# Two halves of the tokens at the first block's first inner norm: a front chain beside the back's last products

## The reference, cut to what matters

```python
mix = jnp.einsum('bsd,de->bse', merged, w_out)
x = x + rmsnorm(mix, g_post_mix)          # the first inner norm
h2 = rmsnorm(x, g_pre_mlp)
a = jnp.square(jax.nn.relu(jnp.einsum('bsd,df->bsf', h2, w_up)))
```

## Time and profile before

| | us |
|---|---|
| median of 3 runs (1938.03 to 1939.36) | 1939.18 |
| the profiled execution's own time | 1938.89 |
| its span, first to last instruction | 1937.2 |
| TensorE (PE) busy in the span | 1902.5 (98%) |
| VectorE (DVE) busy | 1132.7 (58%) |
| ScalarE (ACT) busy | 908.8 (47%) |
| GpSimd (POOL) busy | 85.3 (4%) |

### The profile page before, as it was taken

The page is one execution under the profiler, slowest core; times in us unless marked ns, Lnnn a source line. Parts: engine busy times, 40 slices in busy tenths (PEclk is TensorE's granted clock), DMA queues, the critical chain, the costliest instruction groups (busy, mean ns, idle before and its releaser), DMA issues.

```text
span 1937.2 us, 27051 instructions
## 1 busy us (share of the span) xinstructions
PE 1902.5 (98%) x9061; PEld 1518.7 (78%) x9061; DVE 1132.7 (58%) x1916; ACT 908.8 (47%) x1649; POOL 85.3 (4%) x120
## 2 busy tenths in 40 slices
PE   8999999899999989999999999999999999999998
PEld 7878778688888868757888888888856788888887
DVE  5656566744333357667576656436567667666634
ACT  5555573444433334556544334334466644334433
POOL 2111000000000000110010000000020020000000
PEclk9999999999999999999999999999999999999999
DMA  4222223232333322531233333233441133333222
GB/s 144 66 65 71 66 76 98 65 106 95 98 98 97 95 79 73 115 79 34 82 93 93 98 99 98 95 97 93 109 95 46 41 91 98 103 95 95 93 98 103
DMA packets 169190, 171.29 MB, mean 88 GB/s; under 512 B 48546, under 2 KB 123280, under 8 KB 169104
## 3 DMA queue, kind: packets, MB, share of 16 engines
q1 hardware_dynamic: 169000, 170.14, 30.4%
q10 hardware_dynamic: 104, 0.03, 0.0%
HBM read 159.24 MB, written 2.10 MB: 83 GB/s over the span
## 4 chain that ended last, share of the span: by engine, by line
PE 88%; DVE 6%; ACT 3%; issue 1%; DMA 1%; SPq 0%; POOL 0%; DVEq 0%; ACTq 0%; POOLq 0%
PE bank_b L2185 15%; PE bank_b L2187 15%; PE bank_b L2186 15%; PE bank_a L2185 13%; PE bank_a L2187 12%; PE bank_a L2186 12%; PE bank_b L2559 2%; PE bank_a L2312 1%; PE bank_b L2662 1%; PE bank_a L2643 1%; DVE w_lo L1407 1%; DVE arena L1407 1%; DVE arena L1410 1%; DVE h_lo L1410 0%; DVE x_t L1407 0%
## 5 line engine op out<-in xcount | busy, mean ns | idle before, releaser
L1407 DVE TENSOR_TENSOR w_lo<-w_raw,w_hi 128x512 fp32r<-128x512 f32 (+3 forms) x621 | 414.8, 680 | 584.3 <-ACT w_hi L1124 370.2
L1124 ACT ACTIVATE w_hi<-w_raw 128x512 fp32r<-128x512 f32 (+3 forms) x396 | 233.4, 599 | 441.1 <-PE bank_b L2187 227.2
L2185 PE MATMUL bank_b<-h_hi,w_hi 128*128 128x512 f32 x944 | 371.0, 393 | 1.6 <-DVE w_lo L1407 1.4
L2186 PE MATMUL bank_b<-h_lo,w_hi 128*128 128x512 f32 x944 | 367.7, 390 | 0.0
L2187 PE MATMUL bank_b<-h_hi,w_lo 128*128 128x512 f32 x944 | 367.7, 389 | 0.0
L2185 PE MATMUL bank_a<-h_hi,w_hi 128*128 128x512 f32 x592 | 233.8, 395 | 15.2 <-DVE h_lo L1410 14.3
L829 ACT ACTIVATE w_hi<-w_raw 128x512 fp32r<-128x512 f32 x225 | 137.8, 627 | 232.1 <-PE bank_b L2187 118.6
L2186 PE MATMUL bank_a<-h_lo,w_hi 128*128 128x512 f32 x592 | 232.1, 392 | 0.0
L2187 PE MATMUL bank_a<-h_hi,w_lo 128*128 128x512 f32 x592 | 231.8, 392 | 0.0
L2185 PEld LDWEIGHTS bank_b<-h_hi,w_hi 128*128 128x128 f32 x944 | 177.2, 188 | 40.8 <-issue 3.6
L2186 PEld LDWEIGHTS bank_b<-h_lo,w_hi 128*128 128x128 f32 x944 | 177.2, 188 | 37.2 <-issue 1.4
(11 more groups left out here) (279 smaller groups left out, 2570.0 us busy)
## 6 DMA issues: line engine op xcount, KB each, us to landing
w_raw<-in_w_up_dram SPq DMA_DIRECT2D x240, 256.0 KB, 3.1
w_raw<-in_w_down_dram SPq DMA_DIRECT2D x152, 256.0 KB, 2.6
arena<-arena SPq DMA_DIRECT2D x32, 268.0 KB, 4.3
w_raw<-in_w_in_dram SPq DMA_DIRECT2D x64, 128.0 KB, 2.3
w_raw<-in_w_gate_dram SPq DMA_DIRECT2D x32, 256.0 KB, 2.8
w_raw<-in_w_in_dram SPq DMA_DIRECT2D x32, 256.0 KB, 2.6
w_raw<-in_w_o_dram SPq DMA_DIRECT2D x32, 256.0 KB, 2.6
w_raw<-in_w_out_dram SPq DMA_DIRECT2D x16, 256.0 KB, 2.8
```

The costliest lines, as they stand in the source:

```text
L1124: nc.scalar.activation(w_hi[:, s, 0:c], w_raw[:, s, 0:c], ACT.Copy).then_inc(w_round, 1)
L1407: return nc.vector.tensor_tensor(out_, a, b, op)
L2185: nc.tensor.matmul(out_, a_hi, b_hi, start=start, stop=False, skip_group_check=loose)
L2186: nc.tensor.matmul(out_, a_hi, b_lo, start=False, stop=False, skip_group_check=loose)
```

## The change

The first 256 tokens (front) and the last 256 (back) get a chain of their own. In the second half of the output projection each product of 512 tokens becomes two of 256; `bank_b` is laid out so that banks 0 and 1 hold the front of the four tiles and banks 2 and 3 the back. In the last two chunks the four front pieces come first, then one back piece, the front's sum of squares in three products with ones of 256 columns, then the three other back pieces and the back's sum in five such products. The first group of the up projection takes each chunk as a front and a back half; tiles 0 and 1 of the front stand ahead of tiles 0 and 1 of the back, from tile 2 on both halves follow each other and DVE and ACT work on the whole tile. ACT takes over the variance from DVE. The first three additions of the new squares go from DVE to POOL.

```diff
@@ layout @@
+FRONT, BACK = slice(0, S // 2), slice(S // 2, S)
+        mix_parts_b = bank_b[:, :, :].rearrange("p (h a) n -> p h (a n)", h=2).rearrange("p h (j n) -> p h j n", j=4)
@@ gpsimd @@
+            pool.wait_ge(stat_ready, 1)
+            for t in range(1, 4):
+                pool.wait_ge(sq_ready, KT + t + 1)
+                pool.wait_ge(sq_added, KT - 1 + t - 1)
+                nc.gpsimd.tensor_tensor(ssum[:, :], x_sq[:, 0, :] if t == 1 else ssum[:, :], x_sq[:, t, :],
+                                        ALU.add).then_inc(sq_added, 1)
@@ scalar @@
-            post_squares(range(4, KT), 0, N_UP - 1, 0, 0)
...
+            act.wait_ge(sq_added, 3)
+            for a in range(2):
+                act.wait_ge(front_made, a + 1)
+                nc.scalar.activation(sq[:, a, :], bank_b[:, a, :], ACT.Square).then_inc(front_sq, 1)
+            act.wait_ge(front_stat, 1)
+            act.wait_ge(eps_set, 1)
+            ln_of(FRONT, front_ln)
+            act.wait_ge(front_ln, 1)
+            guess_of(FRONT, front_guess)
+            var_of(FRONT, front_var)
+            act.wait_ge(post_made, 1)
+            nc.scalar.activation(sq[:, 2, :], bank_b[:, 2, :], ACT.Square).then_inc(sq_ready, 2)
+            act.wait_ge(w_used, N_UP)
+            nc.scalar.activation(sq[:, 3, :], bank_b[:, 3, :], ACT.Square).then_inc(sq_ready, 2)
+            round_new(0, FRONT, front_new, front_round)
+            act.wait_ge(stat_ready, 1)
+            ln_of(BACK, ln_ready)
+            act.wait_ge(ln_ready, 1)
+            guess_of(BACK, guess_ready)
+            var_of(BACK, var_ready)
+            round_new(1, FRONT, front_new, front_round)
             split1(N_UP + 2)
-            post_guess(1)
             split1(N_UP + 3)
...
+            for f in range(2):
+                round_new(f, BACK, x_new1, xg_round)
+            for f in range(2):
+                x_square(f)
+            for f in range(2, KT):
+                round_new(f, slice(0, S), x_new1, xg_round)
                 if 3 <= f < KT - 1:
                     split1(N_UP + f + 1)
                 x_square(f)
@@ vector @@
...
+            for f in range(4, 6):
+                add_front(f)
+            dve.wait_ge(front_guess, 1)
+            tt(rs0[:, FRONT], rs1[:, FRONT], rs1[:, FRONT], ALU.mult).then_inc(front_newton, 1)
...
+            inc_new(0, FRONT, front_inc)
+            add_new(0, FRONT, front_inc, front_new)
+            inc_new(1, FRONT, front_inc)
+            lo_new(0, FRONT, front_round, front_ready)
+            add_new(1, FRONT, front_inc, front_new)
+            dve.wait_ge(guess_ready, 1)
...
+            for f in range(2, KT):
+                add_new(f, slice(0, S), xinc_ready, x_new1)
+                if f + 1 < KT:
+                    inc_new(f + 1, slice(0, S), xinc_ready)
+                lo_new(f, slice(0, S), xg_round, xg_ready)
+                if f < KT - 1:
+                    split_lo(N_UP + f + 1)
+            for t in range(4, KT):
+                add_square(t, KT, KT - 1, 1, True)
@@ tensor @@
+            def mix_part(chunks, j, c):
+                r = slice(j * P, j * P + P)
+                for k in chunks:
+                    s = (N_OUT + KT + k) % SLOTS
+                    last = mm3(mix_parts_b[:, 0 if c == FRONT else 1, j, :], w_hi[:, s, r], w_lo[:, s, r], h_hi[:, k, c], h_lo[:, k, c],
+                               k == 0 and j % 2 == 0, k == KT - 1, True)
...
+                mix_part(two, 0, FRONT)
+                mix_part(two, 1, FRONT).then_inc(front_made, 1)
+                mix_part(two, 2, FRONT)
+                mix_part(two, 3, FRONT).then_inc(front_made, 1)
+                mix_part(two, 0, BACK)
+                pe.wait_ge(mix_out, 1)
+                pe.wait_ge(front_added, 2)
+                of_squares(ssum[:, FRONT], FRONT, True, False)
+                pe.wait_ge(front_sq, 2)
+                of_squares(sq[:, 1, FRONT], FRONT, False, False)
+                of_squares(sq[:, 1, BACK], FRONT, False, True).then_inc(front_stat, 1)
+                mix_part(two, 1, BACK).then_inc(post_made, 1)
+                mix_part(two, 2, BACK)
+                mix_part(two, 3, BACK)
...
+            def up1_parts():
...
+                for k in range(2):
+                    pe.wait_ge(front_ready, k + 1)
+                    up_part((N_UP + k) % SLOTS, k, FRONT)
+                for k in range(2):
+                    pe.wait_ge(xg_ready, k + 1)
+                    up_part((N_UP + k) % SLOTS, k, BACK).then_inc(w_used, 1)
+                for k in range(2, KT):
+                    s = use(N_UP + k)
+                    pe.wait_ge(xg_ready, k + 1)
+                    up_part(s, k, FRONT)
+                    up_part(s, k, BACK).then_inc(w_used, 1)
```

More of the change, by code:

```diff
@@ new lines, in round_new @@
+            def round_new(f, c, new, made):
+                act.wait_ge(new, f + 1)
+                nc.scalar.activation(h_hi[:, f, c], x_t[:, f, c], ACT.Copy,
+                                     scale=cols1[:, C_PMLP + f:C_PMLP + f + 1]).then_inc(made, 1)
+            act.wait_ge(sq_added, 3)
[3 more added lines that the diff above has]
+            act.wait_ge(front_stat, 1)
@@ new lines, in lo_new @@
+            def lo_new(f, c, rounded, made):
+                dve.wait_ge(rounded, f + 1)
+                stt(h_lo[:, f, c], x_t[:, f, c], cols1[:, C_PMLP + f:C_PMLP + f + 1],
+                    h_hi[:, f, c].bitcast(F32), ALU.mult, ALU.subtract).then_inc(made, 1)
+            for f in range(4, 6):
+                add_front(f)
+            dve.wait_ge(front_guess, 1)
+            tt(rs0[:, FRONT], rs1[:, FRONT], rs1[:, FRONT], ALU.mult).then_inc(front_newton, 1)
+            dve.wait_ge(front_newton, 1)
@@ L2227, in total_squares, with up_part @@
                     of_last(False).then_inc(stat_ready, 1)
+            def up_part(s, k, c):
+                for j in (0, 2, 3, 1):
+                    if k == 0 and j == 1 and c == FRONT:
+                        pe.wait_ge(ln_ready, 1)
+                        pe.wait_ge(var_ready, 1)
+                    r = slice(j * P, j * P + P)
+                    last = mm3(bank_a[:, j, c], w_hi[:, s, r], w_lo[:, s, r], h_hi[:, k, c], h_lo[:, k, c], k == 0 and c == FRONT,
+                               k == KT - 1, True)
+                return last
@@ new lines, in mix_end, with of_squares @@
+            def mix_end():
+                def of_squares(src, c, start, stop):
+                    return nc.tensor.matmul(bank_a[:, 0 if c == FRONT else 1, c], ones[:, :], src, start=start, stop=stop)
+                two = range(KT - 2, KT)
+                use(N_UP - 1)
+                mix_part(two, 0, FRONT)
[12 more added lines that the diff above has]
+                mix_part(two, 3, BACK)
+                pe.wait_ge(mix_out, 2)
+                pe.wait_ge(sq_added, 3)
+                of_squares(ssum[:, BACK], BACK, True, False).then_inc(sq_added, 1)
+                for a in range(2):
+                    pe.wait_ge(sq_ready, 6 + 2 * a)
+                    for c in (FRONT, BACK):
+                        last = of_squares(sq[:, 2 + a, c], BACK, False, a == 1 and c == BACK)
+                        if a == 1 and c == BACK:
+                            last.then_inc(stat_ready, 1)
+                        else:
+                            last.then_inc(sq_added, 1)
@@ L2416, in _ @@
                     pe.wait_ge(merge_split, k + 1)
[L2417 to L2420, removed]
+                    if half == 0:
+                        wide(bank_a, s, h_hi[:, k, :], h_lo[:, k, :], k == 0, k == KT - 1)
+                    else:
+                        for j in range(4):
+                            mix_part([k], j, FRONT)
+                        for j in range(4):
+                            last = mix_part([k], j, BACK)
+                        last.then_inc(w_used, 1)
+            mix_end()
+            def up1_parts():
+                use(N_UP + 1)
+                pe.wait_ge(mix_out, 4)
+                pe.wait_ge(front_ln, 1)
+                pe.wait_ge(front_var, 1)
+                for k in range(2):
[9 more added lines that the diff above has]
+                    up_part(s, k, BACK).then_inc(w_used, 1)
             def up1(set_, g, i=0, gper=0, late=None):
```

83 lines of the change are left out of this document (65 added, 18 removed).

## The result

| | before | changed |
|---|---|---|
| median of 20 runs, us | 1938.83 | 1942.02 |
| lowest to highest | 1937.12 to 1939.42 | 1940.16 to 1942.79 |
| profiled execution, its span | 1937.2 | 1940.2 |

The ratio is 1.0017 with a 95% interval of 1.0011 to 1.0023: the change costs 3.2 us. The forecast was 1939.6, its range ended at 1942.0. The range missed by 0.02, and the forecast itself by 2.4 us.

What follows compares the result with a forecast made beforehand. PE, busy 98% of the span, was taken as the bound. Old wait and slow clock -9.5, added work +4.3, remaining waits +5.6 gave +0.4 us: median 1939.6, range 1936.4 to 1942.0.

Steps and rivals of the forecast that it cites:

- from there PE bounds the rest as before: After the up projection's first group, nothing more shifts; the stage's +0.4 us carries through to the end.
- SP's load of chunk 6: In the changed stage: moves some 9 us later with a weight split, lands in 3.1, wanted over 8 later, costs nothing.
- The stage itself: Output projection's second half to the up projection's first group's end: +0.4 us in all.
- Halves at 0.120: PE's 256-column products in the changed stage start 0.120 us apart; 192 halved products add 2.56 us of work.
- Rival 2: Halved products in the changed stage cost half, 0.1135 us: -1.4 us, or 1937.8; chance 0.15.
- rival 4: Weight load no longer hides behind 256 columns: 0.168 us a product, 18 us more, 1958; chance 0.05.
- The front chain hidden behind the back's pieces: At the norm, PE's three pieces and five sums cover the front's chain, which uncovered would cost 4.4 us.
- The waits: PE's remaining waits from the norm through the up projection's first group: six terms, 5.6 us together.
- POOL's additions stop DVE: In the up projection's first group, additions on POOL stretch DVE's two-SBUF-input steps, one stop of 1.05 us each.
- rival 1: POOL's additions miss DVE's two-input steps in the first group: -2.1 us, or 1937.1; chance 0.20.
- rival 3: Clock falls to half in the 3.1 us wait before the third chunk: +2.0 us, or 1941.2; chance 0.10.

Runs made afterwards that it cites:

- e12: Kernel before, with PE's code behind the second norm placed at slot 61 of a page of 256; median 1940.73 us against 1938.88.
- e6: Kernel before, with PE's code behind the second norm placed at slot 0 of a page of 256; median 1939.14 us, ratio to before 1.0004.
- e8: Kernel before, with PE's code behind the second norm placed at slot 128 of a page of 256; median 1938.96 us, ratio to before 1.0003.
- e5: Changed kernel, with PE's code behind the second norm placed at slot 0 of a page of 256; median 1940.25 us, ratio to before 1.0011.
- e7: Changed kernel, with PE's code behind the second norm placed at slot 128 of a page of 256; median 1940.28 us, ratio to before 1.0011.
- e2: Changed kernel plus 36 empty PE instructions (semaphore increments) at the second norm; median 1940.35 us, ratio to before 1.0010.
- e1: Changed kernel plus 104 empty PE instructions (semaphore increments) at the second norm; median 1947.0 us, ratio to before 1.0042.
- e4: Like e1, but with the three additions on POOL back on DVE; median 1945.81 us against 1947.0.
- e9: Like e7, but with the three additions on POOL back on DVE; median 1938.55 us, ratio to before 0.9999.

## Why the prediction was wrong

**The term that failed** is the last step of its sum: "from there PE bounds the rest as before". The code there is the same, but not its place. PE's program was 408 instructions longer, its code was loaded at other times, and two of these loads fell on SP while SP's issues set the pace of the second block. That is 1.14 + 0.81 = 1.95 us in the profiles, 1.85 when before alone is put there (e12). No rival named it. "SP's load of chunk 6" was the only place where the prediction looked at SP at all.

**The stage itself** was walked rightly in its mechanism: +0.69 against +0.4 in this pair of profiles. Over the five profiles with the change (88.54 to 89.21) and the four with before's code in this stage (before, e6, e8, e12: 87.85 to 88.54) the means are 0.85 apart, twice the forecast. In part the near sum is luck: PE's waits are 4.7 in total and not 5.6, but the half behind each wait holds up the next by 0.19 to 0.23 in place of 0.12, which was in no term.

- Halves at 0.120: measured 0.119 to 0.120. Rival 2 (0.1135) and rival 4 (the weight load shows) fell. The Trainium skill's page "TensorE: Matmul & The Clock Gate", section "Back-to-back issue gap", gives its 2.5 ns for a product by itself; for these pairs of weight load and product it is too small, the halving costs 12 to 13 ns.
- The front chain hidden behind the back's pieces: yes. PE goes on at 360.53, which is 360.25 in before's count of time, against 360.03.
- The waits, 0.1, 0.3, 0.6, 0.8, 3.1 and 0.7 forecast: 0.24, under 0.1 (the view doesn't list it), 0.27, 0.64, 2.92 and 0.61 measured.
- POOL's additions stop DVE (rival 1 fell): 1.75 to 1.78 a step, 1.05 a stop as taken. The Trainium skill's page "SBUF — State Buffer", section "SBUF: two separate sides", says that such a DVE step and a POOL operation that reads SBUF lock each other out. The trace agrees for DVE: its three steps end 0.54 to 0.55 after POOL's additions, so most of their own 0.69 to 0.75 lies behind them. The third addition too met a step with two SBUF inputs. One row was misread: the step at 970.88 in the earlier trace rows began after POOL's addition had ended (970.40) and shows nothing of operands in PSUM. The one at 969.17 lay beside that addition and took 0.68, so what was read from it holds.
- The clock (rival 3, chance 0.10) falls behind the wait of 2.9 us in 3 of 5 profiles. The chance was too low: it leaned on one profile, in which the clock fell 4.6 us after the sums, and in e6 it fell 2.6 after them. The price was too high: 0.6 and not 1.6, since the slow products lost 1.4 and not 2.3; the later wait took up 0.7 of it, as taken.

**What each part is worth**: the change with the same place of the code 1.1 to 1.3 (e5 less e6, e7 less e8), of which 0.6 to 0.7 stand in the profiles at the first group's sum. The place of the code 1.85 by e12's median, 1.95 by the profiles. Together 3.0 to 3.2, against 3.2 measured. The change's own medians give the place less: it is 3.2 above before, and still 2.0 in e2, e5 and e7, where PE has neither idle time, so 1.2. The rest, 0.7 to 0.9, is what before itself lost at the slots 0 and 128, which is within the noise and stays open. Inside the first part, POOL's additions cost 1.2 to 1.9 (e1 less e4; e7 and e9, each less its before). Without them the change is as fast as before, not faster.

**The range** was built from the stage alone, so its upper end had no room for a cost elsewhere.

## What to carry to other kernels

A change that adds instructions to an engine moves all code behind it. Count the added instructions modulo 256 and look where the loads of code fall then, above all in stretches where the issuing of loads is the bound; to compare two versions of a stage, put what follows at the same slot in both. Before work is moved to shorten a wait, ask which engine bounds the stage once the wait is gone: here it was DVE, whose last step came hardly earlier than before (381.57 in e9, 381.95 in before). And an addition given to POOL isn't free for DVE, but what it costs is decided by who waits for DVE just then.

## What was not expected of the hardware

- A load of 16 KB of PE's code stretched the row that SP was issuing by 0.9 to 1.4 us (2.59 for 1.20, 10.06 for 9.18, 10.03 for 9.16), in all seven places where one fell into the two copies or the fifteen loads behind them.
- Incrementing a semaphore cost PE's queue some 0.14 us each when it stood idle otherwise: 104 made a wait of 7.56 us 14.64 long.
- How long the clock stays at half behind the same gap varies between executions: behind the second norm's 7.56 us of wait, 6 to 12 products.
